# A kernel of transformer blocks on one core: the distance in memory between a pair's second weight tile and the activations it is multiplied with

## The reference

```python
def swiglu(h, w_gate, w_up, w_down):
    return (jax.nn.silu(h @ w_gate) * (h @ w_up)) @ w_down
...
    for l in range(DEPTH):
        x = x + 0.5 * swiglu(rms_norm(x, ffn1_norm[l]), ffn1_wg[l], ffn1_wu[l], ffn1_wd[l])

        h = rms_norm(x, mix_norm[l])
        z = h @ w_in[l]
        ...
        x = x + jnp.concatenate([attn_out, conv_out], axis=-1) @ w_out[l]

        x = x + 0.5 * swiglu(rms_norm(x, ffn2_norm[l]), ffn2_wg[l], ffn2_wu[l], ffn2_wd[l])
    return rms_norm(x, final_norm)
```

## The kernel before, in words

| piece | before |
|---|---|
| any piece at the start of its slot | 64 |
| pair's second, 224 bytes on (224 - 192) | 32 |

## Time and profile before

### The profile page before, as it was taken

One profiled execution on the slowest core, in us unless ns is written; L12 is line 12 of the kernel. 1 busy time (PEld: TensorE's weight loads), 2 busy tenths in 40 slices (PEclk: granted clock), 3 DMA queues, 4 the chain that ended last, 5 costly groups with the idle time before them and its releaser, 6 DMA issues.

```text
span 1244.1 us, 27307 instructions
## 1 busy us (share of the span) xinstructions
PE 1202.5 (97%) x10002; PEld 1161.1 (93%) x10002; DVE 816.5 (66%) x1390; ACT 656.4 (53%) x1121; POOL 166.0 (13%) x228
## 2 busy tenths in 40 slices
PE   6999999999999999999999999999997999998998
PEld 6999999799999999999999799999996887998888
DVE  6766654768666654777665868677656666655664
ACT  5454543556545544555543646555545665655652
POOL 3000000342000000000000351000000000401960
PEclk9999999999999999999999999999997999999999
DMA  7655753455555753655743446556652430543542
GB/s 281 200 180 191 230 175 113 143 166 191 184 187 185 239 166 117 202 189 189 252 167 136 136 159 196 190 195 216 212 169 75 137 126 20 168 155 128 179 153 86
DMA packets 56742, 210.91 MB, mean 170 GB/s; under 512 B 7200, under 2 KB 9280, under 8 KB 56544
## 3 DMA queue, kind: packets, MB, share of 16 engines
q1 hardware_dynamic: 54048, 203.45, 49.3%
q0 software_dynamic: 2480, 6.48, 1.8%
q10 hardware_dynamic: 144, 0.06, 0.0%
HBM read 208.91 MB, written 1.05 MB: 169 GB/s over the span
## 4 chain that ended last, share of the span: by engine, by line
PE 84%; DVE 7%; ACT 3%; issue 3%; POOL 2%; DMA 0%; DVEq 0%; ACTq 0%; SPq 0%
PE bank L1173 25%; PE bank L1175 25%; PE bank L1174 25%; DVE w_lo L748 3%; PE bank L1211 2%; PE bank L1520 2%; PE bank L1500 1%; DVE h_lo L767 1%; ACT w_hi L457 1%; PE bank L1485 1%; DVE probs L886 1%; PE bank L1422 1%; PE bank L1424 1%; PE bank L1423 1%; PE bank L1480 1%
## 5 line engine op out<-in xcount | busy, mean ns | idle before, releaser
L1173 PE MATMUL bank<-h_hi,w_hi 128*128 128x256 f32 (+1 forms) x1992 | 566.8, 285 | 16.8 <-DVE w_lo L748 11.6
L1175 PE MATMUL bank<-h_hi,w_lo 128*128 128x256 f32 (+1 forms) x1992 | 557.9, 280 | 0.0
L1174 PE MATMUL bank<-h_lo,w_hi 128*128 128x256 f32 (+1 forms) x1992 | 557.8, 280 | 0.0
L748 DVE TENSOR_TENSOR w_lo<-w_raw,w_hi 128x1024 fp32r<-128x1024 f32 (+1 forms) x360 | 467.7, 1303 | 75.1 <-ACT w_hi L457 74.9
L457 ACT ACTIVATE w_hi<-w_raw 128x1024 fp32r<-128x1024 f32 (+1 forms) x360 | 397.1, 1108 | 75.9 <-PE bank L1175 58.3
L1173 PEld LDWEIGHTS bank<-h_hi,w_hi 128*128 128x128 f32 x1992 | 377.1, 189 | 24.0 <-issue 19.4
L1175 PEld LDWEIGHTS bank<-h_hi,w_lo 128*128 128x128 f32 x1992 | 379.9, 191 | 0.0
L1174 PEld LDWEIGHTS bank<-h_lo,w_hi 128*128 128x128 f32 x1992 | 377.3, 189 | 0.9
L1173 PE MATMUL bank<-g_hi,w_hi 128*128 128x256 f32 x832 | 232.5, 279 | 1.5 <-DVE g_lo L893 0.8
L1174 PE MATMUL bank<-g_lo,w_hi 128*128 128x256 f32 x832 | 231.7, 278 | 0.0
L1175 PE MATMUL bank<-g_hi,w_lo 128*128 128x256 f32 x832 | 231.7, 278 | 0.0
(11 more groups left out here) (152 smaller groups left out, 1159.5 us busy)
## 6 DMA issues: line engine op xcount, KB each, us to landing
w_raw<-in_w SPq DMA_DIRECT2D x296, 512.0 KB, 3.3
w_raw<-in_wd SPq DMA_DIRECT2D x64, 704.0 KB, 4.1
w_raw<-in_relbias POOLq DMA_DIRECT2D x64, 64.0 KB, 2.3
btab_sb<-in_btab POOLq DMA_DIRECT2D x1, 1536.0 KB, 9.3
x_res<-in_xT SPq DMA_DIRECT2D x2, 512.0 KB, 4.9
out_T<-x_res SPq DMA_DIRECT2D x8, 128.0 KB, 1.7
rope_sb<-in_rope POOLq DMA_DIRECT2D x1, 272.0 KB, 3.9
mats_sb<-in_mats POOLq DMA_DIRECT2D x1, 192.0 KB, 3.8
```

The source lines that it names most:

```text
L748: dve.tensor_tensor(wlo[:, slot, at:at + cols], raw[:, slot, 0:cols], whi[:, slot, at:at + cols].bitcast(F32), ALU.subtract).then_inc(lo_r ...
L1173: pe.matmul(o, h, xh, start=first, stop=False)
L1174: pe.matmul(o, h, xl, start=False, stop=False)
L1175: return pe.matmul(o, lo, xh, start=False, stop=last)
```

## The change

It gives the pair's second piece another place in its slot, a different one for each kind of stage: 8 words (32 bytes) in "gu1", 48 words (192 bytes) in "gu2", 24 words (96 bytes) in "qkv". The second block's first pair takes the place of "gu1". All readers now ask `tile_at`, which also covers slots 2 and 3, where it returns 0, as before. No instruction is added, taken away or moved on any engine: only start addresses differ.

```diff
-ASIDE = 56
+ASIDE = {('gu1', 1): 8, ('gu2', 1): 48, ('qkv', 1): 24}
...
 def tile_at(phase, i):
 
-    return ASIDE if phase in ("gu1", "gu2", "qkv") and i == 1 else 0
+    return ASIDE.get((phase, i), 0)
...
-            def first_pair(ready, q):
+            def first_pair(name, ready, q):
...
-                        mm = product(bank[o][:, 0:T], o, k, *hcols(k), k == 0, k == KT - 1, at=o * ASIDE)
+                        mm = product(bank[o][:, 0:T], o, k, *hcols(k), k == 0, k == KT - 1, at=tile_at(name, o))
...
-                            product(bank[1][:, 0:T], 1, k1, *hcols(k1), k1 == 0, False, at=ASIDE)
+                            product(bank[1][:, 0:T], 1, k1, *hcols(k1), k1 == 0, False, at=tile_at(name, 1))
...
-                    tile8(bank[r][:, 0:T], r)
+                    tile8(bank[r][:, 0:T], r, at=tile_at(name, r))
...
-                                             at=a * ASIDE)
+                                             at=tile_at("gu1", a))
...
-                        mm = product(o[:, 0:TOKENS[kind]], slot, i, *hcols(i, TOKENS[kind]), i == 0, i == KT - 1)
+                        mm = product(o[:, 0:TOKENS[kind]], slot, i, *hcols(i, TOKENS[kind]), i == 0, i == KT - 1,
+                                     at=tile_at("gu1", 2) if piece == 2 else 0)
```

More of the change, by code:

```diff
@@ L1220, in ready @@
                     pe.wait_ge((up_scaled if r % 2 else gate_scaled)[r // 2], n11 + (j + PRIME))
-                first_pair(lambda r: ready(r, 0), q)
+                first_pair(name, lambda r: ready(r, 0), q)
                 for r in (2, 3):
                     ready(r, 0)
-                    tile8(bank[r][:, 0:T], r)
+                    tile8(bank[r][:, 0:T], r, at=tile_at(name, r))
                 with pe.Fori(1, GU // SLOTS) as j:
@@ L1251, in qkv @@
             def qkv(l, q):
-                first_pair(lambda i: pe.wait_ge(lo_ready[PHASES["qkv"].slot(i)], uses("qkv", i, l)), q)
+                first_pair("qkv", lambda i: pe.wait_ge(lo_ready[PHASES["qkv"].slot(i)], uses("qkv", i, l)), q)
                 for i in range(2, QKV):
```

## The result

| | kernel before | changed kernel |
|---|---|---|
| median of 12 runs each, run beside each other | 1252.97 us | 1253.5 us |
| mean | 1250.8 | 1254.3 |
| lowest, highest | 1238.87, 1262.2 | 1246.49, 1261.58 |
| profiled execution | 1245.92 | 1253.43 |

What follows compares the result with a forecast made beforehand. TensorE, busy 97% of the span, bounds the kernel, so the interval between matmuls counts. One slow stretch instead of the profile's two gives 1245.92 - 6.8 = 1239.1, rounded to 1239 us; other parts count nothing; range 1230 to 1260.

Steps and rivals of the forecast that it cites:

- 1536 matmuls times 4.4 ns is 6.8 us: Each long gate and up stretch: 1584 matmuls less the pair's 48, at 117.8 instead of 113.4 ns, costs 6.8 us.
- The levels of none to four slow stretches: Whole execution time by number of slow gate and up stretches: 1232.3, 1239.1, 1245.9, 1252.7, 1259.5 us.
- the 4.4 us kept for a collision at 0 bytes: Second tiles of the pairs: upper bound if only 0 bytes collides; taken as 0, with 4.4 us kept for the range.
- The writers' part: ScalarE and VectorE write the second piece at another place; claimed to cost nothing.
- I expect most stretches to be fast: Four gate and up stretches: one slow of four taken as the forecast case, 1245.92 - 6.8 = 1239.1 us.
- A distance with a rhythm of its own would hand over at a fixed point: From second tile to the 64-byte tiles: the same outcome in both layers, given as reason for expecting fast stretches; 6.8 us each.
- nothing in the trace shows which way that point would fall: The prediction's own objection: the second tile's fixed handover could be to the fast or the slow rhythm; no size given.
- rival 3: Split by stage: gu1 and gu2 one always fast, the other always slow; 1246 us, or 1250 with a collision; chance 0.16.
- rival 1: Distance decides nothing; TensorE's restart moment draws the rhythm; two to three slow stretches, 1246 to 1254 us; chance 0.27 (with rival 4).
- Rival 2: New distances always hand over to the slow rhythm; 6.8 us a stretch, 1259.5 us with all four; chance 0.15.
- 10 slow stretches of 16: Kernel before: three timed runs read as 1, 3 and 4 slow stretches, the profiled one as 2.
- the 0.16 that I gave to times under 1229.2 us: Chance of a measurable gain, about 2% under 1254.28: none slow plus small gains, or kernel before met with four slow.

Runs made afterwards that it cites:

- the second experiment: The changed kernel with gu1's second tile back at 32 bytes (gu2 at 0, qkv at 160): 1250.27 us, ratio 1.0054 against the kernel before.

## Why the prediction was wrong

**What held.** TensorE bounds the kernel, and apart from the clock only the interval between matmuls moved. There are two rhythms, chosen once a stretch, and the step "1536 matmuls times 4.4 ns is 6.8 us" is right: four always slow (1260.14) against four always fast (1233.15, less 0.9 us for the four small matmuls, each of which delays the stream by some 0.22 us: 290.89 to the second product at 291.23, less one interval) is 27.9 us, 7.0 us a stretch. (These two are of different sessions; in one trace it is the 6.9 us above.) In all 17 profiles each of the four stretches kept 113.3 or 117.8 ns over the 1500 intervals that I averaged. The levels of none to four slow stretches, 1232 to 1260 us, are where the runs are, give or take the clock. The second tile itself costs nothing: its pace is 117 to 120 ns at 0, 32, 96 and 160 bytes, 24 x 2 ns at most against the 118 of before, 0.05 us a pair. So the 4.4 us kept for a collision at 0 bytes was not needed. The writers' part held: nothing.

**What failed** is the step "I expect most stretches to be fast", with its reason: "A distance with a rhythm of its own would hand over at a fixed point". That is true of 0 bytes, but the fixed point is the slow one, in all ten profiled stretches right behind it (eight gu2, two gu1), and the timed runs agree (no run of the changed kernel, nor of the second experiment, is at the level of one slow stretch, 1239). I had written myself that "nothing in the trace shows which way that point would fall" and took the favourable side. And it is not true of 96 and 160 bytes, whose patterns remember the entry, so that gu1 stayed a draw: 3 of 8 fast at 96 bytes, where 32 bytes had 5 of 6 in the profiles, too few to tell whether the draw itself leans otherwise. What came out is half of rival 3 (gu2 fixed, on the slow side) with half of rival 1 (gu1 drawn): two to four slow stretches, and 1246 to 1262 us in place of 1239. Rival 2's mechanism, a settled tile that always hands over to the slow rhythm, was the right one for gu2; I gave it 0.15 because I asked for it in all four stretches at once. The sum by my own terms for two stretches fixed slow and two drawn is 1246 to 1260 us.

**A second weakness** is in the base. I read the three timed runs and the profile of before as 10 slow stretches of 16 and so expected that almost any change would help. For that session it was about right: the twelve runs lie near one to four slow stretches, some 31 of 48. But in four further sessions the same kernel had medians of 1246.05, 1243.97, 1239.19 and 1238.76 us. The draw leans differently from session to session (the record names different chips for them, 1, 9, 9 and 10, so it may be the chip), and one session says little about what a stage does on the average. Nor had the 0.16 that I gave to times under 1229.2 us a term of the sum behind it, for that ends at 1232.3. Whether the changed kernel is slower hangs on the session too: not shown beside the 1252.97 us of the first comparison, 1.3% beside the 1238.76 us of the last.

**The rule on two ports.** The Trainium skill, in "TensorE: Matmul & The Clock Gate", "Step-by-step: what each phase is for", has independent read ports for the moving and the stationary operand. By that rule, the prediction said, a relative distance of the two could not matter, which is rival 1. That conclusion is wrong: with the same instructions, 0 bytes against 32 in the second tile moved the median by 16 us (1260.14 against 1243.97 in one session), and the interval patterns change with the place. The page itself is not refuted. Only the weights were moved, so the place of the weight tile may act on its own port, or the two reads may meet somewhere. No run here shows which.

## What to carry to other kernels

When a TensorE-bound kernel has timed runs that fall on evenly spaced levels, count the matmuls in windows of fixed length in each stage before explaining a median, and look at the granted clock for what is left between the levels: one shape with two counts is a stream with two rhythms, and a change that only reshuffles which one is drawn looks like a gain or a loss by chance. Don't tune the draw; put a point into the stream that forgets it, check that its outcome is the fast one, and check by the spread: the kernel before with one 32-column matmul behind each pair has a spread of 4.5 us for the 30 of its neighbour, and the two versions with four fast stretches by such matmuls ran at 0.9973 (0.9949 to 0.9997) and 0.996 (0.9933 to 0.9988) of the kernel before.

## What the runs showed of the hardware that I had not expected

- The place of the weight tile, counted from the activations modulo 256 bytes, sets the pattern of intervals between matmuls of 256 columns (whether the distance or the weights' own place counts is not shown): mean 117 to 120 ns at 0, 32, 96 and 160 bytes, 113.3 or 117.8 at 64. A 64-byte stream keeps what it fell into for over 1500 matmuls.
- A small matmul in such a stream resets it, and its number of columns picks the rhythm: 32 or 96 columns, or two of 128, fast; 64 or 128, slow. In two to eight stretches each there was no exception (32 columns: 8 of 8 fast; 128: 6 of 6 slow; 96 and twice 128: 2 of 2 fast each; 64: 2 of 2 slow). Why these lengths and not others is open, and so is what in the memory or in TensorE makes the patterns.
- What draws the entry is open too. The rows show only that the starts differ by a few ns from the restart on (its first interval is 303 to 313 ns, the next 115 to 122 at 32 bytes), with the same program text.
